# The end of the expert part and the last gate row: how the add-back, the run-time branch and the last norm are cut up

## The reference, cut to what matters

```python
def moe_swiglu(x, router_w, router_b, w_gate_up, w_down):      # 8 experts, top 2
    ...
    for e in range(N_EXPERTS):
        y = y + combine[:, e:e + 1] * swiglu(xf, w_gate_up[e], w_down[e]).astype(F32)
...
        x = layer_norm(DEEPNORM_ALPHA * x + h, ln_ffn_g[i], ln_ffn_b[i])
        x = x + jax.nn.sigmoid(x @ ple_w_gate[i]) * (p[i] @ ple_w_proj[i])
```

## Time and profile before

| | us |
|---|---|
| median of 3 runs (1889.44 to 1892.73) | 1890.29 |
| the profiled execution, its own time | 1890.27 |
| its span, first to last instruction | 1888.5 |
| PE busy | 1834.6 (97%) |
| DVE busy | 1394.3 (74%) |
| ACT busy | 1106.0 (59%) |

### The profile page before, as it was taken

How to read it: one execution, slowest core, us unless ns; L and a number is a source line. 1 busy time by engine, 2 the same in 40 slices (tenths; PEclk the granted TensorE clock), 3 DMA queues, 4 the chain that set the end, 5 groups by cost and what they waited for, 6 DMA issues and landing times.

```text
span 1888.5 us, 24161 instructions
## 1 busy us (share of the span) xinstructions
PE 1834.6 (97%) x9844; PEld 1532.7 (81%) x9853; DVE 1394.3 (74%) x1231; ACT 1106.0 (59%) x989; POOL 61.4 (3%) x83
## 2 busy tenths in 40 slices
PE   8999999999999998899999999999999999999997
PEld 6979997897899876768788888888888888888875
DVE  4766775466645565578988888888888888888876
ACT  4545544374334344357667667676677766776772
POOL 2200000200000001000000000000000000000000
PEclk8999999999999999799999999999999999999998
DMA  7444546432555563049999999999999999999980
GB/s 250 157 153 155 178 167 212 152 129 90 174 188 180 190 206 115 24 163 387 350 367 356 344 371 349 363 363 350 369 359 341 367 352 361 364 336 375 366 307 24
DMA packets 248857, 491.02 MB, mean 260 GB/s; under 512 B 10422, under 2 KB 15610, under 8 KB 248752
## 3 DMA queue, kind: packets, MB, share of 16 engines
q1 hardware_dynamic: 244992, 477.30, 71.3%
q0 software_dynamic: 3328, 10.73, 1.7%
q10 hardware_dynamic: 432, 1.57, 0.2%
HBM read 487.46 MB, written 2.10 MB: 259 GB/s over the span
## 4 chain that ended last, share of the span: by engine, by line
PE 86%; DVE 8%; ACT 2%; DVEq 1%; issue 1%; DMA 0%; ACTq 0%; SPq 0%
PE psum L2518 16%; PE psum L2520 16%; PE psum L2519 16%; PE psum L1974 5%; PE psum L1977 5%; PE psum L1976 5%; PE psum L1920 5%; PE psum L1922 5%; PE psum L1921 5%; PE psum L1994 3%; DVE w_lo L1134 2%; DVE w_lo L1699 1%; ACT w_hi L608 1%; DVE xt_lo L1146 1%; DVE uv L1394 1%
## 5 line engine op out<-in xcount | busy, mean ns | idle before, releaser
L608 ACT ACTIVATE w_hi<-w_raw 128x2048 fp32r<-128x2048 f32 (+1 forms) x357 | 641.6, 1834 | 107.1 <-PE psum L1922 60.2
L1699 DVE TENSOR_TENSOR w_lo<-w_raw,w_hi 128x2048 fp32r<-128x2048 f32 (+1 forms) x238 | 511.5, 2189 | 75.3 <-ACT w_hi L608 75.2
L1134 DVE TENSOR_TENSOR w_lo<-w_raw,w_hi 128x2048 fp32r<-128x2048 f32 (+2 forms) x119 | 261.4, 2228 | 138.5 <-ACT w_hi L608 137.0
L2518 PE MATMUL psum<-w_hi,xg_hi 128*128 128x512 f32 x892 | 357.6, 401 | 1.0 <-DVE w_lo L1699 1.0
L2520 PE MATMUL psum<-w_hi,xg_lo 128*128 128x512 f32 x892 | 353.5, 396 | 0.0
L2519 PE MATMUL psum<-w_lo,xg_hi 128*128 128x512 f32 x892 | 353.5, 396 | 0.0
L1699 DVE TENSOR_TENSOR w_lo<-raw_more,w_hi 128x2048 fp32r<-128x2048 f32 (+1 forms) x118 | 254.6, 2197 | 34.8 <-ACT w_hi L608 34.5
L1974 PE MATMUL psum<-xt_hi,w_hi 128*128 128x256 f32 (+1 forms) x976 | 276.2, 283 | 1.4 <-DVE w_lo L1134 0.6
L1977 PE MATMUL psum<-xt_hi,w_lo 128*128 128x256 f32 (+1 forms) x976 | 275.7, 282 | 0.0
L1976 PE MATMUL psum<-xt_lo,w_hi 128*128 128x256 f32 (+1 forms) x976 | 274.8, 282 | 0.0
L608 ACT ACTIVATE w_hi<-raw_more 128x2048 fp32r<-128x2048 f32 (+1 forms) x118 | 212.7, 1839 | 19.3 <-PE psum L2520 18.5
(11 more groups left out here) (394 smaller groups left out, 2144.1 us busy)
## 6 DMA issues: line engine op xcount, KB each, us to landing
w_raw<-in_moe_w_gate_up SPq DMA_DIRECT2D x150, 1024.0 KB, 7.5
raw_more<-in_moe_w_gate_up SPq DMA_DIRECT2D x74, 1024.0 KB, 7.6
w_raw<-in_moe_w_down SPq DMA_DIRECT2D x64, 1024.0 KB, 7.4
raw_more<-in_moe_w_down SPq DMA_DIRECT2D x32, 1024.0 KB, 7.1
w_raw<-in_w_up SPq DMA_DIRECT2D x22, 1024.0 KB, 5.5
w_raw<-in_ffn_w_gate_up SPq DMA_DIRECT2D x22, 1024.0 KB, 5.5
w_raw<-in_w_in SPq DMA_DIRECT2D x12, 1024.0 KB, 5.7
w_raw<-in_ab_w_in SPq DMA_DIRECT2D x12, 1024.0 KB, 5.3
```

Source lines behind the costliest of these rows:

```text
L608: return act.activation(o, i, func, **kw)
L1134: TT(w_lo[:, k % RING, 0:n], raw(slot, n), w_hi[:, k % RING, 0:n].bitcast(F32), ALU.subtract)\
L1699: TT(w_lo[:, at, 0:n], raw(slot, n), w_hi[:, at, 0:n].bitcast(F32), ALU.subtract).then_inc(S("lo_ready"), 1)
L2518: mm(o, hi[:, q, :], wh, start=(q == first), stop=False)
```

## The change

1. **Overflow items rotated.** ACT and DVE: an item is cut into `item_head` (its 44 chunks and the left half's rows) and `item_end` (four chunks ahead and the right half's rows). The branch now stands between the head of the last item and its end; the end of the last item is written once more behind the branch, as `last_end`.
2. **Last chunks unpadded.** `last_end` rounds and splits the first chunks of `ple1` at their own width (1024 for the projection) and no longer ahead of the branch. On DVE the two gate chunks move behind the second norm, one ahead of tile 1's `xt_lo` and one behind.
3. **Scatter by column halves, the branch between.** `scatter(n, h)` does one column half of both tiles; the left half of the last item stands ahead of the jump, the right one behind it. `added` goes by halves too (four adds of 512 columns in place of two of 1024). The 7 fillers ahead of it are gone.
4. **Last norm's sums by halves.** The left half is added for both tiles as soon as it is there; `add_last` adds the right half of one tile and forms the statistics of left, then right.
5. **Gate row by high weights first.** For the first gate block PE takes, per tile, the products with `w_hi` (16 matmuls, which wait for `hi_ready` alone) and then those with `w_lo` (8). The 6 fillers ahead of it and the wait for `y_added` are gone.
6. ACT copies the first projection block to `p_out` ahead of tile 0's operand and the second behind it.

```diff
-        def last_raw(k, n_items):
+        def last_raw(k, n_over):
 
             at = (IN_ITEMS + k - N_BEFORE_MOE) % RAW_RING
             uses = before_moe[raw_order[at]] + len(range(at, IN_ITEMS, RAW_RING)) + (k - N_BEFORE_MOE) // RAW_RING + 1
-            return raw_order[at], 16 * (uses - N_EXP * uses_in_item(at)) + 16 * uses_in_item(at) * n_items
+            return raw_order[at], 16 * uses + 16 * uses_in_item(at) * n_over
...
-                    round_to(blocks[0][1] + RING, r)
-                    for block_ in blocks[0:2]:
-                        projected(*block_)
+                    projected(*blocks[0])
                     turned(m, 0)
                     turned(m, 1)
+                    projected(*blocks[1])
...
-                for n in range(2):
-                    end = MOE_UP_CHUNKS + len(MOE_DOWN) * (n + 1)
-                    rounds(k, end + 2, i)
-                    k = end + 2
-                    wait_used(act, c0 + end, r)
-                    copy(ys_hi[:, n * NB:(n + 1) * NB], psum[:, 4 + n, :], scale=gslot[:, 0:1])\
-                        .then_inc(S("ys_hi_ready"), 1)
-                rounds(k, k + 2, i)
...
+                end = MOE_UP_CHUNKS + len(MOE_DOWN)
+                rounds(k, end + 2, i)
+                wait_used(act, c0 + end, r)
+                item_rows(0)
+                rounds(end + 2, MOE_CHUNKS, i)
+
+            def item_rows(n):
+                copy(ys_hi[:, n * NB:(n + 1) * NB], psum[:, 4 + n, :], scale=gslot[:, 0:1]).then_inc(S("ys_hi_ready"), 1)
+
+            def item_end(i):
+
+                rounds(MOE_CHUNKS, MOE_CHUNKS + 2, i)
+                wait_used(act, N_BEFORE_MOE, (i + 1) * R_ITEM)
+                item_rows(1)
+                rounds(MOE_CHUNKS + 2, MOE_CHUNKS + 4, i)
+
+            def last_end():
+
+                c0 = chunk0["ple1"]
+                round_to(c0 + 2, n_items * R_ITEM)
+                wait_used(act, N_BEFORE_MOE, n_items * R_ITEM)
+                item_rows(1)
+                round_to(c0 + 4, n_items * R_ITEM)
...
+                n_over = act.value_load(route_i[0:1, 4:5], min_val=0, max_val=ITEMS - N_EXP)
+                for i in range(1, N_EXP - 1):
                     item(i)
+                item_head(N_EXP - 1)
 
                 def overflow(i):
                     with act.If(n_items > i):
-                        item(i)
+                        item_end(i - 1)
+                        item_head(i)
                         if i + 1 < ITEMS:
                             overflow(i + 1)
                     act.end_ifs()
 
                 overflow(N_EXP)
                 me.cap = N_STATIC
+                last_end()
                 root_tile(0)
             if "ple1" in live:
-                me.chunk += RING
...
-                    round_to(blocks[0][1] + RING, r)
                     turned(m, 0)
                     turned(m, 1)
                     normalize(1, m, y)
                     dve.sem_inc(S("gain_used"), 2)
+                    round_to(blocks[0][1] + 3, r)
                     turned(m, 2)
                     turned(m, 3)
+                    round_to(blocks[0][1] + 4, r)
                 else:
                     round_to(blocks[0][1] + 4, r)
...
-            def added(n, t):
-
-                dve.wait_ge(S("scattered"), 2 * n + t)
-                TT(y[:, t, :], y[:, t, :], psum[:, 4 + 2 * t:6 + 2 * t, :].rearrange("p b n -> p (b n)"), ALU.add)\
-                    .then_inc(S("y_added"), 1)
+            def added(n, h, tiles=range(NT)):
+
+                dve.wait_ge(S("scattered"), 2 * n + h)
+                cols = slice(h * NB, (h + 1) * NB)
+                for t in tiles:
+                    i = TT(y[:, t, cols], y[:, t, cols], psum[:, 4 + 2 * t + h, :], ALU.add)
+                return i
 
             def scattered(n):
 
-                for t in range(NT):
-                    added(n, t)
+                for h in range(2):
+                    added(n, h).then_inc(S("y_added"), 1)
+
+            def add_last(t):
+
+                added(n_items, 1, (t,))
+                dve.bn_stats(bn[:, t, 0, :], y[:, t, 0:NB])
+                dve.drain()
+                dve.bn_stats(bn[:, t, 1, :], y[:, t, NB:D])
...
+            def last_end():
+
+                round_to(chunk0["ple1"] + 2, n_items * R_ITEM)
+                dve.wait_ge(S("ys_hi_ready"), 2 * n_items)
+                item_rows(1)
...
                 overflow(N_EXP)
                 me.cap = N_STATIC
-
-                def add_last(t):
-
-                    added(n_items, t)
-                    dve.drain()
-                    for h in range(2):
-                        dve.bn_stats(bn[:, t, h, :], y[:, t, h * NB:(h + 1) * NB])
-
+                last_end()
+                added(n_items, 0)
+                dve.drain()
                 add_last(0)
                 normalize(0, 10, y)
                 add_last(1)
             if "ple1" in live:
                 r = n_items * R_ITEM
-                me.chunk += RING
                 ple(1, 10, r)
...
+            def rows_high_first(bl, m, src, rc):
+
+                bb, cc, n0, n, ps = bl
+
+                def high(i, t):
+                    pe.wait_ge(S("hi_ready"), cc + i + 1 + RING * rc)
+                    for k in range(4 * i, 4 * i + 4):
+                        w_ = w_hi[:, (cc + i) % RING, (k - 4 * i) * n:(k - 4 * i + 1) * n]
+                        mm(acc[bb % 2][t][:, 0:n], xh(k, t), w_, start=(k == 0), stop=False)
+                        mm(acc[bb % 2][t][:, 0:n], xl(k, t), w_, start=False, stop=False)
+
+                def low(i, t):
+                    pe.wait_ge(S("lo_ready"), RING + cc + i + 1 + RING * rc)
+                    for k in range(4 * i, 4 * i + 4):
+                        w_ = w_lo[:, (cc + i) % RING, (k - 4 * i) * n:(k - 4 * i + 1) * n]
+                        m_ = mm(acc[bb % 2][t][:, 0:n], xh(k, t), w_, start=False, stop=(k == KD - 1))
+                    return m_
+
+                high(0, 0)
+                high(1, 0)
+                turn_tile(m, src, 1)
+                low(0, 0)
+                pe.wait_ge(S("xt_ready"), 4 * m + 4)
+                high(0, 1)
+                high(1, 1)
+                low(0, 1).then_inc(S("w_used"), 1)
+                low(1, 0)
+                low(1, 1).then_inc(S("w_used"), 1)
...
-                    pe.wait_ge(S("y_added"), 2 * n_items + 2)
-                    keep_warm(6)
                 pe.wait_ge(S("xt_ready"), 4 * m + 2)
                 wait_acc(blocks[2][0])
-                rows_chunk(blocks[2], 0, xh, xl, r, tiles=(0,), mark=None)
-                turn_tile(m, x, 1)
-                rows_chunk(blocks[2], 1, xh, xl, r, tiles=(0,), mark=None)
-                pe.wait_ge(S("xt_ready"), 4 * m + 4)
-                for j in range(2):
-                    rows_chunk(blocks[2], j, xh, xl, r, tiles=(1,))
+                if i:
+                    rows_high_first(blocks[2], m, x, r)
+                else:
+                    rows_chunk(blocks[2], 0, xh, xl, r, tiles=(0,), mark=None)
+                    turn_tile(m, x, 1)
+                    rows_chunk(blocks[2], 1, xh, xl, r, tiles=(0,), mark=None)
+                    pe.wait_ge(S("xt_ready"), 4 * m + 4)
+                    for j in range(2):
+                        rows_chunk(blocks[2], j, xh, xl, r, tiles=(1,))
...
-            def scatter(n):
-
-                pe.wait_ge(S("ys_ready"), 2 * n)
-                for t in range(NT):
-                    for h in range(2):
-                        for q, part in enumerate((ys_hi, ys_lo)):
-                            m = mm(psum[:, 4 + 2 * t + h, :], selt[:, t * P:(t + 1) * P], part[:, h * NB:(h + 1) * NB],
-                                   start=(q == 0), stop=(q == 1))
-                    m.then_inc(S("scattered"), 1)
+            def scatter(n, h):
+
+                pe.wait_ge(S("ys_ready"), 2 * n - 1 + h)
+                for t in range(NT):
+                    for q, part in enumerate((ys_hi, ys_lo)):
+                        m = mm(psum[:, 4 + 2 * t + h, :], selt[:, t * P:(t + 1) * P], part[:, h * NB:(h + 1) * NB],
+                               start=(q == 0), stop=(q == 1))
+                m.then_inc(S("scattered"), 1)
...
-                        if h == 0 and j == 0 and not first and i != N_EXP:
-                            scatter(i)
+                        if h == 0 and j == 0 and not first:
+                            for half in range(1 if i >= N_EXP else 0, 2):
+                                scatter(i, half)
...
-                keep_warm(7, 0)
-                scatter(N_EXP)
+                scatter(N_EXP, 0)
 
                 def overflow(i):
                     with pe.If(n_items > i):
                         item(i)
+                        scatter(i + 1, 0)
                         if i + 1 < ITEMS:
                             overflow(i + 1)
-                        if i == N_EXP:
-                            scatter(n_items)
```

(1 more changed line is left out.)

44 lines of the change are left out of this document (28 added, 16 removed).

## The result

The changed kernel takes 1880.8 us (median of 6 runs, 1877.61 to 1884.16) against 1890.97 us for the kernel before in the same comparison (6 runs, 1887.9 to 1892.96): a ratio of 0.9949, 95% interval 0.9933 to 0.9964. The forecast was 1882.5 us, with a range of 1879.3 to 1886.0.

The account below looks back on a forecast made before the run. PE bounds the items and DVE's chain the last 52 us. A new timeline of that end, tile 1 turned at 1854.7 against 1863.2 and the span ending at 1880.7, plus 1.8 us around it, gave 1882.5 us; range 1879.3 to 1886.0.

Parts of the forecast that it names:

- What bounds the kernel: PE, busy 97% of the span, never pausing in the items; narrower adds there cost DVE 0.4 us per item, hidden.
- PE's jump: PE's branch over the overflow items, between scatter halves: 3.4 us, from 2.4 to 4.8, since weights are still landing.
- The clock: In the pause at PE's branch the granted clock falls to 1.2 GHz, adding 1.6 us over the 28 matmuls behind.
- PE is later now: At tile 0's turn PE's matmuls end 0.8 us after DVE has tile 0 ready; before, DVE was later by 6.3.
- DVE's and ACT's jumps cost nothing: Ahead of the last item's end, up to 4.4 us of DVE's branch and 5.2 of ACT's are free.
- (b): DVE's 3.1 us pause is a wait on a register-held count, not the branch: at worst 1884.9 us; chance 0.03.
- (e): DVE's branch is not hidden while weights land, so PE waits for `ys_lo`: 1883.7 to 1886.7 us; chance 0.06.
- Chunks out of the way: Two padded and two gate chunks leave DVE's path: 9.0 us less 2.3, with the branch's 3.1 most of the gain.
- Gate row by high weights first: At tile 1's turn: four matmuls move ahead, worth 0.9 us, but `xt_lo` comes 3.3 us behind it; alone loses.
- (c): PE's branch over the overflow items is cheap, 2.4 us, and the clock holds: 1881.0 us; chance 0.12.
- (a): First rival: clock falls again in the pause behind tile 0's turn, costing up to 1.6 us: 1883.8 us; chance 0.13.
- (d): Without fillers PE stays at 1.2 GHz to the end, the gate's 96 matmuls costing 18.5 us: about 1901; chance 0.03.

Follow-up runs that it names:

- experiment 9: Changed kernel with four extra 1 MB memory-to-memory transfers issued by SP behind the last weights, loading DMA through PE's jump: tail 44.11 us against 43.9.
- experiment 1: Changed kernel with DVE's jump over the overflow items put back behind the last item's end, ahead of the adds: tail 45.41 us against 43.9.
- experiment 4: Changed kernel with PE scattering nothing ahead of its jump, both column halves behind it: tail 44.76 us against 43.9.
- experiment 3: Changed kernel with PE scattering both column halves ahead of its jump, so the jump stands behind the scatter: tail 46.62 us against 43.9.
- Experiment 2: Changed kernel with DVE splitting the two gate chunks ahead of the left half's add again, not behind the second norm: tail 48.18 us against 43.9.
- experiment 7: Changed kernel with the two projection chunks rounded and split at 2048 columns again, behind the jump: tail 44.60 us against 43.9.
- Experiment 5: Changed kernel with DVE splitting the first gate chunk in its pause behind the left adds, the second ahead of tile 1's `xt_lo`: tail 43.20 us against 43.9.
- experiment 8: Kernel before the change without its 7 and 6 filler matmuls, nothing else changed: tail 54.31 us against 52.59.

## Why the prediction was right, point by point

- **What bounds the kernel.** Held. The items gain and cost nothing: PE is busy 120.0 of 120.0 us there, and the four narrower adds per item leave no wait. They cost DVE less than the 0.4 us per item that the forecast had reckoned: four take 2.47 us, where two wide ones took 2.35. The gain lies behind E: 52.59 to 43.94, 8.65 us, where the forecast had 7.8.
- **PE's jump: the term that was mis-sized.** 3.4 us forecast, 2.40 measured; the bound of 2.4 was right and the step towards SP's 4.8 us was not. The sign that the forecast named, a pause of 3 to 4 us behind the first four scatter matmuls, did not come: it was 2.01. What failed is "a jump under load": experiment 9 holds the load and the jump stays at 2.5. What SP's 4.8 us consist of stays open; a part of it may be a wait for DVE, as the forecast allowed.
- **The clock.** Forecast: it falls once, in the pause at the jump, and costs 1.6 us over 28 matmuls, which take 8.1 us. Measured: it falls once, to 0.50 for 3.4 us, and from the right half's start to the turn pass 8.2 us. After the turn it held, through a pause of 1.65 us. By the rule that the turn does not count as work for the clock (the Trainium skill, "TensorE: Matmul & The Clock Gate", Part 4, PE-mode transpose), the pause would have been some 2.7 us, more than the 2.0 at which the clock fell at the jump, and the first rival follows; it did not happen in this kernel. The clock at 1.2 GHz was confined to the stretch behind the jump. No run here isolates the rule, since experiments 1 and 4, where the clock fell there, had longer pauses by either count. That it held in the changed kernel was forecast as likely, and not shown by any row.
- **"PE is later now" than DVE.** Held, by 1.1 us (tile 0 normed at 10.38, turned at 11.51); experiment 3 shows it from the other side, where an earlier norm bought nothing.
- **DVE's and ACT's jumps cost nothing.** Held. ACT's took 3.4 us of its cover of 5.2, DVE's idle time of 3.18 ends with ACT's rounding, and `ys_lo` comes at 1.15 us behind E as before. Had DVE's stayed behind `last_end`, it would show (experiment 1). Rivals (b) and (e) are out.
- **Chunks out of the way.** The forecast put most of the gain here. Experiment 2 gives back 4.2 us with two of the four chunks, experiment 7 gives 0.7 for the padding of the other two. That one is small because PE's jump covers most of it. The 4.2 us hold what a second low stretch of the clock, of 6.8 us, took as well. No run isolates the last norm's sums by halves or ACT's new order for `p_out` (parts 4 and 6 of the change).
- **Gate row by high weights first.** The forecast said that `xt_lo` of tile 1 comes 3.3 us behind the turn with four matmuls to fill them; it came 3.16 behind it, and PE paused 0.98 us (some 2 forecast) ahead of those four. The forecast had them fill the wait from its start; the profile shows that they wait for DVE's split themselves (`w_lo`, line 1157), done at 20.0, and still end when `xt_lo` comes, so this cost nothing. That the part "alone loses" was argued and not tested. Experiment 5 does not test it, since a split still stands ahead of `xt_lo` there. What the rows show is small: from tile 1's turn to the last gate matmul pass 20.88 us in after and 20.37 before. The high-first order with everything else as before was not run.
- **Rival (c)**, a cheap jump with a clock that holds, was half true: the jump was cheap, the clock fell. **(a)** did not come in the changed kernel, but a second low stretch or a later one came in three variants (experiments 1, 2, 4), whose tails are 0.8 us and more above, so it was rightly in the range. **(d)**, slower, had nothing to it: the longest low stretch behind E in any run was 13.7 us, in the kernel before without its fillers.
- **The total.** The medians of the two comparisons differ by 10.2 and 10.4 us, the tails by 8.7 (before's from one execution). The changed kernel's forecast used the profiled execution of before as its base, whose time is within 0.02 us of that kernel's median. The last 1.5 us are not in the items behind the first one's up and gate part. From its first down product to E the two kernels take the same 915.35 us, and the next row but one of PE's timeline stands 914.8 us ahead of E in all thirteen profiles. First before, then after:

```profile
920.59 0.47 PE L2518 MATMUL psum<-w_hi,mh_hi 128*128 128x512 f32 x1 [0.22 <-DVE w_lo L1699]
...
916.58 0.47 PE L2596 MATMUL psum<-w_hi,mh_hi 128*128 128x512 f32 x1
```

So they lie ahead of 920 us, where the clock's low stretches fall, and E varies by 6.7 us from run to run. One pair with the same low time of 44.4 us (experiments 8 and 1) has E 0.56 us apart. Whether that part is the diff's or chance stays open. The run-to-run spread is also larger than the forecast allowed: it gave it one us, and the changed kernel's six runs reach from 1877.61 to 1884.16. That the median came within 1.7 us of 1882.5 is partly luck; the tail, 43.9 us where 44.8 was forecast, is the better test, and there the difference is the jump.

## What to carry to other kernels

The run-time branch that is jumped over cost PE, DVE and ACT 2.1 to 3.7 us each here, and PE the same with the DMA engines idle or busy; put such a branch on each engine where that engine waits anyway, and let the last item's end be written out again behind it. When an engine waits at the end of a phase, look first for work of the next phase queued ahead of the critical step, and move it behind. Once the waits are short the next limit is the clock that they leave behind, so compare variants by where it fell, and by a tail measured from a common instruction rather than by the whole time.
